# Two transformer blocks in one launch: another order of the second stage, combine weights spread by four products, idle products in two waits

## The reference

```python
# block 1: attention, then a mixture of 32 experts (2 of 8 in one of 4 groups per token)
y = y + combine[:, e:e + 1] * (silu(t @ w_gate[e]) * (t @ w_up[e]) @ w_down[e])      # width 512
# block 2, layer 0: conditioned attention with a Fourier branch; layer 1: short convolution
sh_m, sc_m, g_m, sh_f, sc_f, g_f = split(silu(cond) @ ada_w[l] + ada_b[l], 6)
x = x + g_m * mixer(modulate(x))
x = x + g_f * ec_moe(modulate(x))     # 16 experts of width 1024, 32 tokens each, scattered back by weight
```

## Time and profile before

| what | value |
|---|---|
| median of 3 runs | 1934.58 us (1933.48 to 1935.50) |
| the profiled execution, its own time | 1933.05 us |
| its span, first to last instruction | 1931.2 us |
| mean granted TensorE clock | 0.877 |
| TensorE busy | 1463.3 us, 76% |
| VectorE, ScalarE, GpSimd busy | 489.4, 239.3, 83.1 us |
| read from memory | 714.75 MB, 371 GB/s over the span |
| chain that ended last | DMA 53%, PE 35%, DVE 4%, issue 4%, POOL 2%, ACT 1% |

### The profile page before, as it was taken

The page is one execution under the profiler, slowest core; times in us unless marked ns, Lnnn a source line. Parts: engine busy times, 40 slices in busy tenths (PEclk is TensorE's granted clock), DMA queues, the critical chain, the costliest instruction groups (busy, mean ns, idle before and its releaser), DMA issues.

```text
span 1931.2 us, 28874 instructions
## 1 busy us (share of the span) xinstructions
PE 1463.3 (76%) x12714; PEld 804.3 (42%) x12714; DVE 489.4 (25%) x970; ACT 239.3 (12%) x584; POOL 83.1 (4%) x92
## 2 busy tenths in 40 slices
PE   9898986767788798899656656656999766656665
PEld 5445642333334363656323323224866432323322
DVE  4774421111121058843001000003553100000001
ACT  2222210111211122321000000001001000000000
POOL 2210000000000032100000000000000000000000
PEclk9999998898898999899878778788999877888777
DMA  9544999999999986568999999999997999999997
GB/s 360 216 187 162 366 401 422 419 420 420 420 417 417 401 332 240 186 287 367 424 420 421 421 419 424 420 420 398 355 363 286 417 424 419 420 424 418 422 420 290
DMA packets 123089, 717.73 MB, mean 372 GB/s; under 512 B 5968, under 2 KB 10832, under 8 KB 98384
## 3 DMA queue, kind: packets, MB, share of 16 engines
q1 hardware_dynamic: 121536, 713.11, 90.8%
q10 hardware_dynamic: 1424, 2.71, 0.4%
HBM read 714.75 MB, written 1.05 MB: 371 GB/s over the span
## 4 chain that ended last, share of the span: by engine, by line
DMA 53%; PE 35%; DVE 4%; issue 4%; POOL 2%; ACT 1%; SPq 0%; ACTq 0%; DVEq 0%; POOLq 0%
DMA ring<-in_moe_w_down 22%; DMA ring<-in_moe_w_up 17%; DMA ring<-in_w_down 14%; PE bank L1670 5%; PE bank L2537 4%; PE bank L505 4%; PE bank L1622 3%; PE bank L1613 2%; PE bank L946 2%; PE bank L339 2%; PE bank L977 1%; PE bank L649 1%; DMA ring<-in_w_gate 1%; PE bank L2295 1%; PE bank L1696 1%
## 5 line engine op out<-in xcount | busy, mean ns | idle before, releaser
L1622 PE MATMUL bank<-ring,arena 128*32 128x256 f32 x3968 | 294.0, 451 | 159.7 <-DMA ring<-in_moe_w_up 103.6
L1670 PE MATMUL bank<-ring,arena 128*32 128x256 f32 x2912 | 245.1, 494 | 172.4 <-DMA ring<-in_moe_w_down 135.3
L1622 PEld LDWEIGHTS bank<-ring,arena 128*32 128x32 f32 x3968 | 144.6, 125 | 289.6 <-issue 107.2
L1670 PEld LDWEIGHTS bank<-ring,arena 128*32 128x32 f32 x2912 | 117.1, 136 | 289.4 <-issue 179.5
L1613 PE MATMUL bank<-ring,arena 128*32 128x512 f32 x976 | 134.6, 665 | 59.7 <-DMA ring<-in_w_up 31.3
L505 PE MATMUL bank<-ring,low 128*128 128x512 f32 (+1 forms) x352 | 153.1, 585 | 0.0
L1742 DVE TENSOR_TENSOR arena<-arena,bank 128x128 f32<-128x128 f32 (+1 forms) x64 | 22.7, 354 | 502.3 <-PE bank L1622 498.9
L1696 PE MATMUL bank<-arena 32*128 32x256 f32 x1024 | 95.6, 444 | 16.6 <-PE bank L1696 10.6
L505 PEld LDWEIGHTS bank<-ring,low 128*128 128x128 f32 x352 | 66.2, 195 | 68.2 <-issue 67.3
L1748 ACT ACTIVATE arena<-bank 128x256 f32<-128x256 f32 x64 | 24.6, 384 | 561.3 <-PE bank L1683 558.3
L1757 DVE TENSOR_TENSOR arena<-bank,gate_strips 128x256 f32<-128x256 f32 x32 | 13.6, 425 | 305.7 <-PE bank L1670 305.7
(11 more groups left out here) (315 smaller groups left out, 1373.3 us busy)
## 6 DMA issues: line engine op xcount, KB each, us to landing
ring<-in_moe_w_up SPq DMA_DIRECT2D x64, 2048.0 KB, 26.8
ring<-in_moe_w_gate SPq DMA_DIRECT2D x60, 2048.0 KB, 25.5
ring<-in_moe_w_down SPq DMA_DIRECT2D x60, 2048.0 KB, 26.9
ring<-in_w_up SPq DMA_DIRECT2D x31, 2048.0 KB, 25.4
ring<-in_w_down SPq DMA_DIRECT2D x31, 2048.0 KB, 26.0
ring<-in_w_gate SPq DMA_DIRECT2D x30, 2048.0 KB, 25.3
ring<-in_ada_w SPq DMA_DIRECT2D x24, 2048.0 KB, 13.0
ring<-in_attn_w_in SPq DMA_DIRECT2D x8, 2048.0 KB, 20.8
```

What stands on the lines that cost most here:

```text
L1622: last = nc.tensor.matmul(GU[up][32 * j:32 * j + 32, 0:QW], xgT[:, x + kk, a:a + C], w[:, kq, j * QW:(j + 1) * QW], start=(kk == 0), stop= ...
L1670: last = nc.tensor.matmul(z_bank(M)[32 * j:32 * j + 32, 0:QW], act_s[:, b, q * C:(q + 1) * C], w[:, kq, j * QW:(j + 1) * QW], start=(kk == ...
```

## The change

Five steps of `steps2()` move, one semaphore wait is for one less, `wsel` is written once and not four times, `w_turn_pe` makes the four strips by four products in place of one transposition per tile of tokens, and `keep_pe` comes into the router of the second stage (7 products) and between the two halves of the last down product of mixtures 2 and 3 (8 products). The seventh entry added to `FILL`, 12, is used nowhere.

```diff
-FILL = (20, 5, 5, 25, 26, 14)
+FILL = (20, 5, 5, 25, 26, 14, 12, 7, 8)
-        IDLE = [bank[2], bank[5], bank[3]]
+        IDLE = [bank[2], bank[5], bank[3], bank[0]]
-        wsel = carve(2 * T, GE * 4 * C)
+        wsel = carve(2 * T, GE * C)
...
                     tr_pe(i, t, out_ready(m, t), banks)
+                    if m == 1:
+                        keep_pe(FILL[7])
...
-            for t in range(T):
-                bt = (g % 2) * T + t
-                last = v.tensor_tensor(wsel[:, bt, :].rearrange("p (e j c) -> p e j c", e=GE, j=4),
-                                       sel[:, bt, :].rearrange("p (e c) -> p e c", c=C).unsqueeze(2).broadcast_to([P, GE, 4, C]),
-                                       weight[:, t, :].unsqueeze(2).unsqueeze(2).broadcast_to([P, GE, 4, C]), ALU.mult)
-            last.then_inc(M.wsel, 1)
+            v.tensor_tensor(four(wsel[:, b, :]), four(sel[:, b, :]), weight.unsqueeze(3).broadcast_to([P, T, GE, C]),
+                            ALU.mult).then_inc(M.wsel, 1)
...
                 i = place_down(M, e, part)
+                if M.stage > 1 and e == M.ne - 1 and part:
+                    keep_pe(FILL[8], 3)
...
-            g, a = e // GE, (e % GE) * 4 * C
+            g, a = e // GE, (e % GE) * C
...
-                last = nc.tensor.transpose(WT[:, t * P:(t + 1) * P], wsel[:, (g % 2) * T + t, a:a + 4 * C], ident)
+                for j in range(4):
+                    last = nc.tensor.matmul(WT[32 * j:32 * j + 32, t * P:(t + 1) * P], wsel[:, (g % 2) * T + t, a:a + C], ident,
+                                            start=True, stop=True)
...
             if b == 0:
-                nc.tensor.wait_ge(h2["vput"], 6)
+                nc.tensor.wait_ge(h2["vput"], 5)
...
                 if u != 10:
                     yield "ada_sum", (u + 3) // 2
-                yield "ada_add", 2
                 if u != 10:
                     yield "ada_use", (u + 3) // 2
+                yield "ada_add", 2
                 yield "proj", (u, (1,))
                 yield "tr", u - 1
                 yield "sum", u
+                if u > 8:
+                    yield from attend2(s + 1)
                 yield "ada_add", 1
                 yield "gain", u
-                if u > 8:
-                    yield from attend2(s + 1)
                 yield "ada_add", 2 if u == 8 else 1
...
             yield "fourier_proj", 1
+            yield "fourier_first", 0
             yield from attend2(9)
             yield "ada_add", 3
-            yield "fourier_first", 0
             yield "fourier_chan", 0
```

## The result

| | before | after |
|---|---|---|
| median | 1934.03 us (1932.54 to 1935.50, 4 runs) | 1919.66 us (1917.43 to 1920.81, 4 runs) |
| ratio | | 0.9924, 95% interval 0.9907 to 0.9942 |
| profiled execution, own time and span | 1933.05, 1931.2 us | 1920.81, 1918.7 us |
| mean granted clock | 0.877 | 0.885 |
| TensorE, VectorE busy | 1463.3, 489.4 us | 1455.8, 475.8 us |

The change is faster, and the median fell by 14.4 us. To see where, I cut each span at five instructions that all kernels have: the first gather of each mixture, the sum over partitions of job 5 (A, the start of the moved steps) and the first output projection (B, behind them).

The account below looks back on a forecast made before the run. Weights' DMAs bound mixtures 1 and 2, TensorE's waits and clock the second stage. Terms -16.1 - 0.8 + 0.5 + 2.1 = -14.3 us gave a median of 1920.3 us, range 1915 to 1927.

Parts of the forecast that it names:

- What bounds it: Weights' DMAs bound mixtures 1 and 2, TensorE the second stage; time lost there delays mixture 2 one for one.
- Rival C: Second stage not on the path, since weights set mixture 2's full rate: gain swallowed, +2, 1937 us; chance 0.08.
- The second stage, -16.1: Moved steps there: -12.7 us of TensorE waits, -8.3 of lower clock, +4.9 of new waits; ends -10 and -19.
- The new waits: Second stage, TensorE: turn of unit 7, two conditioning sums, turn of unit 11, scores 10 with next product; 4.9 us together.
- the 1.6 before the turn of unit 11: Second stage: TensorE free at 780.5, rotation ready at 782.1 because maxima now stand ahead of `gain`; 1.6 us wait.
- rival A: VectorE becomes the bound or the 1.6 us wait lowers the clock: stage gives 10, total -8.5, 1926 us; 0.19 with another rival.
- the prediction's own signs of being wrong: Waits above 2 us before the turn of unit 10 or 11, an unmoved 889, or a longer mixture 1.
- The router, -0.8: Second stage's router, seven idle products: -1.7 us if they hold the clock, +1 to +1.9 if not; -0.8 taken.
- The combine weights, +0.5: `w_turn_pe`, eight products for two transpositions: +0.46 us per expert, mostly in free TensorE time; +0.5 at mixture 1's start.
- Rival D: Strips run one behind the other and TensorE becomes mixture 1's bound: +17 us in total, 1952 us; chance 0.05.
- The estimate in the prediction by the figure of the Trainium skill: Combine weights without the four times faster FP32 transpose mode: +1.2 us per expert, +5 over mixture 1's start.
- The end, +2.1: Last down product of mixture 3: eight idle products as plain cost, +1.9 us (ends -1 and +4); +2.1 with the turn.

Follow-up runs that it names:

- two executions: The changed kernel, profiled in the main comparison and once more unchanged: A to B 85.2 and 84.3 us, medians 1919.66 and 1917.12 us.
- the second: The changed kernel run again as it is, beside the kernel before: 1917.12 us, ratio 0.9919.
- order only: Kernel before with only the moved steps and the wait for one less copy, no strips or new idle products: 1920.30 us, ratio 0.9931.
- the first comparison: The changed kernel against the kernel before, four runs each: 1919.66 against 1934.03 us, ratio 0.9924.

## Why the prediction was right

**What bounds it.** Right. Mixtures 2 and 3 kept their lengths within 1.5 us, and the gain between A and B came through to the median. Rival C (hidden) falls.

**The second stage, -16.1.** It gave -13.9 and -14.7 in two executions. The waits removed went as forecast; each move has its own run for it. The new waits were forecast as 0.7, 1.3, 0.6, 1.6 and 0.7 and came as 0.74, 1.44, 0.74, 2.54 and 0.21 in the first execution, and with 0.99 for the last in the second. The mis-sized term is the 1.6 before the turn of unit 11: it came 0.9 longer in both. In the first execution the clock also fell to its lower level behind it, as rival A had it (4.92 for a projection of 3.62), and the stage gave 2.2 less than forecast; in the second it did not fall, and the stage gave 1.4 less. A wait above 2 us before that turn was among the prediction's own signs of being wrong. It came, and the total held because the other waits went as said. Rival A's terms add up to -8.2 and not -8.5, which changes no bound.

The cause of the 0.9 is in GpSimd's timeline. I took 3.76 from `gain` to the end of the rotation. Before:

```profile
763.41 2.60 POOL L277 TENSOR_TENSOR small<-small,columns 128x8 f32<-128x8 f32 x1 [27.68 <-DVE small L267]
767.61 2.19 POOL L587 TENSOR_TENSOR arena<-arena,room 128x128 f32<-128x128 f32 x4 [1.60 <-DVE arena L563]
```

After, GpSimd, and below it VectorE:

```profile
778.72 1.64 POOL L277 TENSOR_TENSOR small<-small,columns 128x8 f32<-128x8 f32 x1 [6.27 <-DVE small L267]
783.62 3.17 POOL L587 TENSOR_TENSOR arena<-arena,room 128x128 f32<-128x128 f32 x4 [3.26 <-DVE arena L563]
```
```profile
778.55 1.28 DVE L2166 TENSOR_REDUCE small<-bank 128x1 f32<-128x512 f32 x2
782.06 0.69 DVE L557 TENSOR_TENSOR arena<-bank,small 128x512 f32<-128x512 f32 x1
784.18 1.48 DVE L409 SCALAR_TENSOR_TENSOR room<-ring,condT,room 128x1024 f32<-128x1024 f32 x1
```

`gain` starts at 782.06 and the rotation ends at 786.79: 4.73. The rotation takes 3.17 instead of 2.19, and now runs beside an add (784.18) and no longer beside the maxima. With the scores put back behind `gain`, it was 2.19 again, and of all 14 profiled executions the three with `gain` ahead have 2.18 or 2.19 and the eleven others 3.16 to 3.18. So the order sets this length; that it is the add beside it is read from the rows.

**The router, -0.8.** It gave -1.9 in both executions of after, and about -0.3 in seven of the nine others. So my upper end, +1 to +1.9 where the clock falls, was wrong: in five of the seven the idle products took over the slow stretch that tile 1 had before. The mean of the eleven is near -0.8 by luck, and no execution showed it.

**The combine weights, +0.5 and +0.46 of busy time per expert.** No cost was measured, and the busy time rose by (45.5 - 30.8) / 64 = 0.23. The price was too high because I used busy time per call for pieces that overlap what follows. A call of `sums_pe` is busy 0.47, but eight strips cost 0.44 from start to start at full clock, and the two transpositions that they replace 0.37: +0.07 per expert. Rival D falls with the 0.44. The estimate in the prediction by the figure of the Trainium skill (TensorE: Matmul & The Clock Gate, Terms), four times 0.40 for the eight, falls with it too.

**The end, +2.1.** Wrong, by 3.5 us: the stretch from mixture 3 to the end became 1.4 shorter. I read that both halves' weights had landed, and so took the idle products as plain cost (+1.9). In before, the weights of the second half landed 2.1 us after the first half began. Counted from the first gather of mixture 3, the second half begins at 441.7 to 441.9 with the idle products in after, and at 441.2 to 441.7 in the four kernels without them whose first half was fast. So they cost a few tenths at most. And of the 6.00 that I took as the end's usual length, 2 were a slow clock that is often not there: order only, without idle products, has an end of 452.2 us, where before has 454.3. Whether idle products there make a slow end, of more than 454 us, rarer (one of nine executions with them, two of five without) is too few to say. The small share for the last turn was not measured.

**The sum.** -14.3 forecast, -14.4 by the medians of the first comparison and -17.0 by the second, whose intervals overlap. In the profiled pair it is -12.2, since stage one took 3.9 longer there with unchanged code; without that it is -16.1. So the stage's -16.1 was 2 too good, and the rest, forecast as +1.8, came as -2.2, 4 too bad: 3.5 of it by the end and 1.1 by the router, less what the other stretches differ by. The mechanism held for the stage, which is nearly all of the change. That the total fell within 1 us was luck in part: errors of opposite signs.

## What to carry to other kernels

In a list that several engines walk in one order, price each move by the wait it removes and the lower clock behind that wait, and then walk the list again for the engine that is nearly full: what counts there is what stands ahead of the step that others need, more than its busy sum. When taking one late step away gains nothing, try it together with the next late one before giving it up. Price short matmuls from the start of a piece to the start of the next, since the busy time of a piece includes an end that the next one covers. Before calling extra work plain cost, look when the weights for the next piece land: a slow piece ahead can hide a wait that is there in other executions.

## What the runs showed of the hardware that was not expected

**GpSimd and VectorE slow each other.** The rotation on GpSimd (four instructions) took 2.19 us beside maxima that read PSUM and 3.17 beside an add that reads two operands from SBUF; the root took 2.60 beside an add and 1.64 beside maxima; the add itself took 1.48 and 1.47 beside the rotation, and 1.28 to 1.3 otherwise. For the rotation and the root the same pairs came back in all 14 profiled executions, by their order. The Trainium skill (SBUF — State Buffer, SBUF: two separate sides) says that VectorE with two SBUF inputs and a GpSimd operation that reads SBUF exclude each other for a whole instruction. The direction of these rows agrees with it; the pairing was read from the timelines and not tried by itself.

**The clock's share varies with unchanged code.** Stage one, whose instructions are the same in all kernels, took 212.1 to 216.0 us in 14 profiled executions. In the profiled executions of before and after it was 212.1 at a mean clock of 0.94 and 216.0 at 0.92, with TensorE busy 192.0 and 196.2 us and VectorE 129.4 and 129.5. In the second stage's router the seven idle products, behind the same list of instructions, took 1.73 us in six executions and 3.0 to 3.2 in five. One profiled pair can thus hide or feign 4 us of a change; lengths of stages separate the two, and a median over several runs averages them out.
